# Register work for the down product placed at the head of each pass of the expert loop

## The reference

```python
scores = sigmoid(h @ router_w)                     # (tokens, 64)
# group-limited choice of 8 experts of 64 for each token, weights w
for each expert e, for its tokens:                 # EXPERT_HIDDEN = 256
    hid = silu(xb @ w_gate[e]) * (xb @ w_up[e])    # 1024 -> 256
    y   = hid @ w_down[e] * w                      # 256 -> 1024
# y is summed back per token; one shared expert is added
```

## Time and profile before

| | |
|---|---|
| median of three runs | 1974.98 us |
| profiled execution, its time | 1974.16 us |
| its span | 1972.2 us |
| PE busy | 1737.7 us (88%) |
| DVE, ACT, POOL busy | 853.8, 599.5, 243.4 us |
| up and gate matmuls, L1328 | 4160, 504.5 us |
| down matmuls, L1353 | 2048, 248.0 us |
| DMA | 552.02 MB, mean 280 GB/s |

### The profile page before, as it was taken

How to read it: one execution, slowest core, us unless ns; L and a number is a source line. 1 busy time by engine, 2 the same in 40 slices (tenths; PEclk the granted TensorE clock), 3 DMA queues, 4 the chain that set the end, 5 groups by cost and what they waited for, 6 DMA issues and landing times. The chain is left out here.

```text
span 1972.2 us, 40674 instructions
## 1 busy us (share of the span) xinstructions
PE 1737.7 (88%) x12455; PEld 738.3 (37%) x12456; DVE 853.8 (43%) x2899; ACT 599.5 (30%) x1239; POOL 243.4 (12%) x254
## 2 busy tenths in 40 slices
PE   4999689888989999989997579959799999999997
PEld 3545554432333333333332355535433333333332
DVE  2255683453545545545554525645422232232223
ACT  2142372222333333333332204224122222222232
POOL 0002300002222222222221000230000000000000
PEclk8999799988999999999998879969899999999998
DMA  9214710457999999999955753461589999999980
GB/s 338 99 64 158 270 66 1 192 189 268 404 413 413 398 392 389 413 397 380 371 205 223 287 179 107 180 248 34 203 317 414 394 367 414 414 414 413 414 333 21
DMA packets 155442, 552.02 MB, mean 280 GB/s; under 512 B 21001, under 2 KB 25837, under 8 KB 138489
## 3 DMA queue, kind: packets, MB, share of 16 engines
q1 hardware_dynamic: 132704, 507.10, 65.7%
q0 software_dynamic: 15984, 42.18, 5.7%
q10 hardware_dynamic: 6696, 1.98, 0.4%
HBM read 536.11 MB, written 24.25 MB: 284 GB/s over the span
## 5 line engine op out<-in xcount | busy, mean ns | idle before, releaser
L1328 PE MATMUL bank<-arena 128*32 128x512 f32 x4160 | 504.5, 603 | 25.8 <-issue 12.4
L1353 PE MATMUL bank<-arena 128*32 128x512 f32 x2048 | 248.0, 598 | 29.3 <-issue 28.6
L1328 PEld LDWEIGHTS bank<-arena 128*32 128x32 f32 x4160 | 112.6, 109 | 234.8 <-issue 222.9
L1875 DVE COPY arena<-arena 128x12 bf16 (+1 forms) x270 | 53.5, 198 | 254.8 <-issue 254.8
L1930 DVE TENSOR_TENSOR arena<-arena,bank 64x512 f32<-64x512 f32 x130 | 88.5, 681 | 152.9 <-ACT arena L957 151.0
L979 ACT ACTIVATE arena<-bank 128x128 f32<-128x128 f32 x128 | 35.5, 277 | 392.0 <-PE bank L1394 372.1
L988 ACT ACTIVATE arena<-bank 128x512 f32<-128x512 f32 x128 | 76.4, 597 | 223.9 <-PE bank L1353 223.9
L1072 PE MATMUL bank<-arena 128*128 128x512 f32 (+3 forms) x384 | 130.2, 500 | 11.7 <-DVE arena L1549 11.7
L730 POOL DMA_INDIRECT yrows<-arena x80 | 81.1, 1013 | 411.1 <-ACT arena L988 411.1
L1318 PEld LDWEIGHTS bank<-arena 128*128 128x128 f32 x528 | 74.2, 210 | 111.3 <-issue 109.6
L1353 PEld LDWEIGHTS bank<-arena 128*32 128x32 f32 x2048 | 56.7, 109 | 154.1 <-issue 150.7
(11 more groups left out here) (332 smaller groups left out, 1980.0 us busy)
## 6 DMA issues: line engine op xcount, KB each, us to landing
arena<-in_exp_w_gate SPq DMA_DIRECT2D x128, 1024.0 KB
arena<-in_exp_w_up SPq DMA_DIRECT2D x128, 1024.0 KB
arena<-in_exp_w_down SPq DMA_DIRECT2D x128, 1024.0 KB
arena<-in_w_ada SPq DMA_DIRECT2D x10, 3072.0 KB, 12.5
arena<-in_w_ada SPq DMA_DIRECT2D x8, 2048.0 KB, 13.9
arena<-in_w_in SPq DMA_DIRECT2D x8, 2048.0 KB, 9.5
arena<-yrows SPq DMA_DIRECT2D x16, 1024.0 KB, 18.4
arena<-in_w_out SPq DMA_DIRECT2D x4, 2048.0 KB, 9.9
```

The source lines that it names most:

```text
L1328: ins = pe.matmul(bank[0][r:r + UNIT, :], XGT[:, c, hh, un, :], wv[un][:, :, hh, c, :], start=(c == 0), stop=(c == 3))
L1353: ins = pe.matmul(bank[2][r:r + UNIT, :], HIDT[:, c, UNIT * un:UNIT * un + UNIT], wv[un][:, c, cg * 512:(cg + 1) * 512], start=(c == 0), s ...
```

## The change

In each pass the register work of step (5) is written at the head, in front of the wait for `a_xe`, and so are the two lines that take the half and the parity of b for step (4).

```diff
                 with pe.Fori(0, blocks) as b:
                     word = pe.snap(word_next)
                     e, slot, step = experts_of(word)
+                    now, slot_now, step_now = experts_of(pe.snap(word_now))
+                    pe.reg_mov(word_now, word)
+                    pe.reg_mov(word_next, experts_word(b + 2))
+                    if not last:
+                        half = pe.snap(b // 2)
+                        odd = pe.snap(b % 2)
                     pe.wait_ge(a_xe, b + 2)
                     if last:
                         pick_and_gather(b + 3)
@@
                     if last:
                         turn_tokens(0, b + 3)
                     else:
-                        half = pe.snap(b // 2)
-                        odd = pe.snap(b % 2)
                         with pe.If(odd == 0):
                             turn_tokens(0, half * 16 + 32)
                         with pe.Else():
                             turn_tokens(1, half * 16 + 32)
-                    now, slot_now, step_now = experts_of(pe.snap(word_now))
-                    pe.reg_mov(word_now, word)
-                    pe.reg_mov(word_next, experts_word(b + 2))
                     if last:
                         pe.wait_ge(a_y, b + 2)
                         pe.wait_ge(v_ow, b + 1)
```

## The result

The changed kernel takes 2005.11 us in the median of four runs (2003.24 to 2006.67); the kernel before, run beside it, 1975.6 (1974.53 to 1976.67). The ratio is 1.0156, with a 95% interval of 1.0144 to 1.0169: 29.5 us slower. The forecast was 2000. The profiled execution's span is 2002.6 us, 30.4 more than before.

The account below looks back on a forecast made before the run. PE bounds the kernel, with its sequencer setting the time at the head of layer-0 passes. The terms, 56.7 - 10.3 - 6.6 - 15.9 + 1 = 24.9 us on 1974.16, give 1999.1, forecast as 2000; range 1984 to 2020.

Parts of the forecast that it names:

- (a): Head of layer-0 passes: 0.80 us of added sequencer work, mostly uncovered, mean 0.727 us in 78 passes, +56.7 us.
- (b): Layer 0, PE's waits for up weights: they shrink when PE is slower, -10.3 of 10.6 us.
- (c): Layer 0, before the down product: the late or long table load no longer holds it in 11 passes, -6.6 us.
- (d): Layer 0, hidden copy: 33 copies held until a gather ends become less late as the turning comes later, -15.9 us.
- the rival in which (d) brings nothing: Layer 0: hidden copies stay as late as before, so the loss is 40.8 us, time 2016; chance 0.22.
- (e): Layer 1: a margin of about 1.0 us at the head covers the added 0.80 us, so 0.
- (f): Head: table loads that take long, up to 1158 ns, now stand where nothing covers them, +1 us.
- The clock: Layer 0: no cost, since it is 1.00 with idle times up to 1.9 us, longer than a pass will have.
- The deep queue: Layer-0 head: a 64-instruction queue would hide the added work behind the down product, leaving -6.6 us, 1968.4; chance 0.05.

Follow-up runs that it names:

- load_head: Kernel before, with only the table load and its checks moved to the head, the word moves left before the down product: 1994.98 us, ratio 1.0128.
- words_mid: Kernel before, with the whole register work moved between the up product and the turning of the tokens: 1961.87 us, ratio 0.9953.
- load_twice: Changed kernel with a second load of the same table word and its checks at the head: 2098.09 us, ratio to the kernel before 1.0649.
- before_again: The kernel before, unchanged, run and traced once more on another occasion: 1967.4 us.
- words_head: Kernel before, with only the moves of the words put at the head, the table load left before the down product: 1969.75 us, ratio 0.9997.
- gather_late: Kernel before, with POOL's layer-0 gather also waiting for the turning of its pass's hidden rows: 1989.98 us, ratio 1.0101.

## Why the prediction was right, and where its terms were off

**Direction, place and mechanism** were as forecast: the sequencer sets the time at the head of a layer-0 pass, the waits for `a_xe` and `v_gu` cover none of the added work, and the place decides. load_head, words_mid and the dose in load_twice show it, each against a rival.

**(a) The head was undersized.** From the down product's first weight load to the add with the wait for `a_xe` it is 0.99 us before and 1.87 after, so the change adds 0.87 to 0.88 us and not 0.80. The missing part is the fused operation, which I had put at 0.05: the longer of the two in a pass went from 52 to 162 ns, so the arithmetic that is fused in is not free. 0.07 us in 78 passes is 5 us. The loop's fused operations over the whole run, before and after:

```profile
L1433 PEldq FUSED_REGOPS  x256: 37/48/52, 432.2 to 1955.1; - x128
```

```profile
L1433 PEldq FUSED_REGOPS  x256: 37/102/178, 433.0 to 1985.5; - x128
```

**(b) The weight waits** vanished, 10.6 to 0. (a) and (b) together were to be +46.4 and came to +55.0. The 5 us above are a part of that; where the other 3 arise is not shown.

**(c) and (d) together** were to be -22.5 and came to -18.7. On the pair where no copy is late there is only (c), and it is -9.3 (11.2 to 1.9), against -6.6. If (c) was about the same on the first pair, (d) brought some 9 us there and not 15.9.

**(d) was a property of that occasion, not of the program.** In the first pair the lateness did shrink: the starts beyond 0.48 us after the turning add up to 25.0 us before (33 passes) and 10.3 after (25 passes), where the forecast leaves 5.6. The changed kernel's trace keeps the link that I had read: in its 25 late passes the copy starts 1.4 to 1.7 us after the gather began, as here:

```profile
521.15 1.02 POOL L711 DMA_INDIRECT arena<-hrows,arena  x1 [0.32 <-issue]
521.64 0.45 PE L1394 MATMUL bank<-arena 64*128 64x64 f32 x2
...
522.75 0.28 ACT L979 ACTIVATE arena<-bank 128x128 f32<-128x128 f32 x1 [3.81 <-PE bank L1394]
```

But in before_again gathers stand beside the turning in the same way and no copy is late, so the start of a gather beside the turning is not enough to cause it. My rule for the short delays was loose too: in the kernel before a gather 0.09 us behind the turning goes with a copy after 0.84 us (turning at 488.97) and after 1.56 (547.32). What delays the signal is open.

Without any late copy the loss was 34.4 us, not the 40.8 of the rival in which (d) brings nothing. There the kernel before runs into the weights more (18.1 us of waits instead of 10.6), which the slower one gets back. The ratios of the two pairs, 1.0144 to 1.0169 and 1.0142 to 1.0178, overlap, so the runs don't show that the late copies changed the loss at all. That the sum needed (d) to come near 2005 is luck: it took off 15.9 us where other terms were too small.

**(e) Layer 1** is right to the pass: no idle at 0.87 us in the 46 passes with a margin, and 20.9 us in the same 46 when the load is doubled.

**(f) is wrong in sign.** The long loads vanished at the head (longest 334 ns) instead of standing uncovered. They go with the places where the up product is queued in front of them. All loads of words_head, words_mid and load_head, in this order:

```profile
L1359 PEldq TENSOR_LOAD <-arena x132: 297/303/1140, 424.7 to 1949.3; - x132
```

```profile
L1359 PEldq TENSOR_LOAD <-arena x132: 296/302/1008, 425.0 to 1940.8; - x132
```

```profile
L1359 PEldq TENSOR_LOAD <-arena x132: 296/302/324, 425.3 to 1966.1; - x132
```

Why, no run here tells.

**The sum.** -18.7 and +55.0 make 36.3; from the first to the last turning of layer 0 the traces differ by 34.4 us (608.2 and 642.6). Some 4 us come back outside the loop, 1.9 before its first turning and 2.1 between the two loops, which I did not pursue; 30.4 of span remain. So the waits of layer 0 grew by 11 us more than the terms add up to (36.3 against 24.9), and 6 us came back where the sum had nothing. The miss of 5 us is what is left of both, and smaller than the misses in it: the time came nearer than its terms, and that too is luck.

**The clock** was no cost, as forecast (1.00 over the loop), though the ground that I gave was not quite right: the longest idle time was 2.4 us, at the start of the loop, and not below 1.9.

**The deep queue.** The head was not hidden: 0.87 us in 79 passes is 69 us, and the idle that is put down to issue there rose by 65.6. The Trainium skill, "TensorE: Matmul & The Clock Gate", table of specs, gives TensorE's queue a depth of 64. Read plainly that would have hidden the head, and the trace doesn't agree with this reading; how many places one of this kernel's matmuls takes in such a queue, no run here shows.

## What to carry to other kernels

An engine's register work, table loads and branches take their time from one sequencer, and what they cost depends on how far it is ahead of its array at that place. Read its own records at both places before moving anything: here 0.87 us a pass cost 30 us at the head of a layer-0 pass, where the branches still have to be done before the up product can start, and nothing in layer 1, where matmuls follow the head at once, or behind the queued up product. A position in front of a wait is free only if the sequencer would have stood in that wait. A cover of 1.0 us in one loop and none in the other, in the same source lines, is why one number for "the loop" would have misled.

## What the runs showed that I had not expected

- **The clock fell at idle times of about 2 us.** In load_twice the granted clock was 0.93 to 0.97 of 2.4 GHz over the long stretches of layer 0 shown above, since some passes ran partly at the lower level of 1.2 GHz. In the pass whose window shows 0.84, the first 24 up matmuls took 4.48 us instead of 2.78, after 2.01 us of idle. The changed kernel, with 0.95 us of idle a pass there, had 1.00, and so did the kernel before through four passes with 1.6 to 1.9 us of idle; so the length of one idle time alone doesn't decide it.
- **A table load on PE's sequencer** takes 0.30 us in most passes; behind the queued up product some took up to 1158 ns, at the head none over 334.
- **Matmuls that waited for a gather held the sequencer** and with it the branches behind them, while the array was still busy: 21.5 us in gather_late, by the pass shown and 42.6 us of idle against 12.4.
- **PE's signal for the turned hidden rows can come up to 1.1 us late** on one occasion, in 33 of 80 passes, all of one parity, and in none on two others, with the same program. The ends of matmuls are modelled, so the traces don't tell whether the matmuls or only their signal were late.
